# A hybrid decoder step on one core: where the SBUF arrays begin

## The reference

```python
h = rmsnorm(x, w_norm_mix)
proj = jnp.einsum('bld,de->ble', h, w_in)                  # 2048 -> 6160
o_r, s_ret = retention_chunkwise(q_r, k_r, v_r, s_ret0)
o_g, s_gla = gla_chunked(q_g, k_g, v_g, log_a, s_gla0)
x = x + jnp.einsum('ble,ed->bld', jnp.concatenate([o_r, o_g], -1), w_out)

q = jnp.einsum('td,de->te', rmsnorm(x, w_norm_ffn), w_pq)  # product-key queries
s1, s2 = q_first @ sub_keys1, q_second @ sub_keys2         # 128 + 128 keys, 8 heads
eidx, gate = top 16 of the 16 x 16 best sums, softmax
u = u_tab[eidx]
act = gelu(einsum('thkd,td->thk', u, xb))
out = einsum('thk,thkd->td', gate * act, v_tab[eidx])
y = rmsnorm(x + out, w_norm_final)
```

## Time and profile before

| | us |
|---|---|
| median of 3 runs | 3749.38 |
| lowest, highest | 3748.39, 3750.2 |
| the profiled execution | 3746.15 |
| its span, first to last instruction | 3744.4 |
| TensorE busy | 3542.5 (95%) |
| VectorE busy | 2554.4 (68%) |
| ScalarE busy | 1285.9 (34%) |
| mean granted TensorE clock | 0.964 |

### The profile page before, as it was taken

One profiled execution on the slowest core, in us unless ns is written; L12 is line 12 of the kernel. 1 busy time (PEld: TensorE's weight loads), 2 busy tenths in 40 slices (PEclk: granted clock), 3 DMA queues, 4 the chain that ended last, 5 costly groups with the idle time before them and its releaser, 6 DMA issues. The chain is left out here.

```text
span 3744.4 us, 50131 instructions
## 1 busy us (share of the span) xinstructions
PE 3542.5 (95%) x19479; PEld 3299.2 (88%) x19479; DVE 2554.4 (68%) x3619; ACT 1285.9 (34%) x1610; POOL 927.2 (25%) x609
## 2 busy tenths in 40 slices
PE   8999999676997998999999999999899999999996
PEld 6888888555786878999999999999899999999996
DVE  4112221786323216999999888887789899898997
ACT  5112221333322313323325777774222222222222
POOL 0000000000000000033333333432445445454452
PEclk9999999677998999999999999999999999999998
DMA  5222330543523405487888999999898998989986
GB/s 205 90 112 109 118 114 26 187 149 110 214 87 141 150 33 202 171 326 306 321 327 327 383 386 381 385 387 371 338 370 351 377 357 360 367 351 377 360 344 246
DMA packets 187000, 965.64 MB, mean 258 GB/s; under 512 B 18658, under 2 KB 61346, under 8 KB 86099
## 3 DMA queue, kind: packets, MB, share of 16 engines
q1 hardware_dynamic: 108082, 506.07, 35.7%
q0 software_dynamic: 61264, 426.27, 29.4%
q10 hardware_dynamic: 17488, 31.06, 2.3%
HBM read 865.77 MB, written 97.55 MB: 257 GB/s over the span
## 5 line engine op out<-in xcount | busy, mean ns | idle before, releaser
L1802 PE MATMUL hidden_hp<-dense_hi,units_whi 128*128 128x384 f32 x2048 | 696.6, 340 | 2.5 <-ACT units_whi L1565 2.5
L1803 PE MATMUL hidden_hp<-dense_lo,units_whi 128*128 128x384 f32 x2048 | 688.7, 336 | 0.0
L2284 PE MATMUL outputs_vp<-outputs_w_hi,units_whi 128*128 128x384 f32 x2032 | 679.0, 334 | 0.5 <-DVE units_wlo L1569 0.4
L2286 PE MATMUL outputs_vp<-outputs_w_hi,units_wlo 128*128 128x384 f32 x2032 | 678.7, 334 | 0.0
L2285 PE MATMUL outputs_vp<-outputs_w_lo,units_whi 128*128 128x384 f32 x2032 | 678.7, 334 | 0.0
L1565 ACT CAST units_whi<-units_raw 128x2048 fp32r<-128x2048 f32 x214 | 410.8, 1920 | 768.5 <-PE outputs_vp L2286 609.2
L1744 POOL DMA_INDIRECT hidden_row<-u_rows,expert_ids x192 | 367.4, 1914 | 999.5 <-DVE dots L2027 629.3
L1569 DVE TENSOR_TENSOR units_wlo<-units_raw,units_whi 128x2048 fp32r<-128x2048 f32 x214 | 489.9, 2290 | 102.1 <-ACT units_whi L1565 100.7
L2220 DVE SCALAR_TENSOR_TENSOR accg<-outputs_row,outputs_w_op,accg 128x2048 f32<-128x2048 f32 x192 | 450.9, 2349 | 51.1 <-DMA outputs_row<-v_rows,outputs_id 48.4
L2027 DVE CUSTOM_DVE_ANT_0 hidden_row<-hidden_row,hidden_h_row 128x2048 f32<-128x2048 f32 x192 | 436.7, 2290 | 70.9 <-DMA hidden_row<-u_rows,expert_ids 68.4
L2082 POOL DMA_INDIRECT outputs_row<-v_rows,outputs_id x192 | 319.6, 1664 | 525.3 <-DVE accg L2220 476.4
(11 more groups left out here) (366 smaller groups left out, 4821.2 us busy)
## 6 DMA issues: line engine op xcount, KB each, us to landing
units_raw<-v_units SPq DMA_DIRECT2D x128, 1024.0 KB
units_raw<-u_units SPq DMA_DIRECT2D x86, 1024.0 KB
in_proj_raw<-w_in SPq DMA_DIRECT2D x48, 1024.0 KB, 5.9
hidden_raw<-u_units SPq DMA_DIRECT2D x42, 1024.0 KB
hidden<-hidden_hid SPq DMA_DIRECT2D x128, 192.0 KB
gate_mat<-units_big SPq DMA_DIRECT2D x12, 2048.0 KB, 22.6
units_big<-hidden SPq DMA_DIRECT2D x16, 1536.0 KB
units_big<-gate_mat SPq DMA_DIRECT2D x16, 1536.0 KB
```

Of the source, the lines that this page charges most:

```text
L1802: mm(o, un.hi[s][:, x, :], h_hi[:, x, :], start=x == 0, stop=False)
L1803: mm(o, un.hi[s][:, x, :], h_lo[:, x, :], start=False, stop=False)
L2284: mm(o, un.hi[x][:, at, :], W_hi[s][:, e, :], start=e == 0, stop=False)
L2286: ins = mm(o, un.lo[x][:, at, :], W_hi[s][:, e, :], start=False, stop=e == CH - 1)
```

## The change

`squares` becomes a view of an array of 32 words, 128 bytes, so everything behind it begins 32 bytes later. On the right side an array `edge` of 32 bytes is made first, so the two `dense` arrays begin 32 bytes earlier. The instructions on each engine and their order are the same as before.

```diff
-        ident, squares = sb("ident", [P, P]), sb("squares", [P, D // NB, TILES])
+        ident = sb("ident", [P, P])
+        squares = sb("squares", [P, 32])[:, 0:D // NB * TILES].rearrange("p (b t) -> p b t", t=TILES)
...
         with ExitStack() as rows:
+            rows.enter_context(nc.sbuf_tensor("edge", [P, 8], F32, side="right"))
             dense = [rows.enter_context(nc.sbuf_tensor(f"dense_{p}", [P, KT, ND], F32R, side="right")) for p in ("hi", "lo")]
```

## The result

The changed kernel has a median of 3754.76 us against 3748.44 for the kernel before, measured beside it in 19 runs each; the ratio is 1.0019 with a 95% interval of 1.0012 to 1.0026. So the change costs about 7 us, 0.19%: inside the forecast's own range (3742 to 3756), but the forecast said that nothing would be measured, and the interval leaves out 1. The runs also lie further apart than before: 3751.19 to 3764.62 us against 3744.09 to 3751.87.

The account below looks back on a forecast made before the run. TensorE, busy for 3542.5 of 3744.4 us, was taken as the bound, with VectorE and DMA close behind. The four terms summed to 0, so 3749 us, unchanged; own range 3742 to 3756, range that should hold the time 3722 to 3760.

Parts of the forecast that it names:

- Term 1: Full-precision matrix multiplies on TensorE, some 2,800: placement costs 0; even 1 ns each would be 3 us.
- Term 2: Rounded 4-byte multiplies of projections, hidden and output stages, 16,700: gain bounded at 179 us, loss put at 0, taken as 0.
- Term 3: VectorE and ScalarE operations: placement costs 0 in both directions; 2 ns per ScalarE instruction would be 3 us.
- Term 4: DMA loads and stores: taken as 0, with at most 2.6 us of gain counted, in the query loads.
- A: Rival: the fixed part of the rounded multiplies, 10.7 ns each, is all placement; faster, 3610 us; chance 0.07.
- B: Rival: a ninth of the rounded multiplies' 10.7 ns goes, eight 64-byte pieces instead of nine; 20 us faster, 3729 us; chance 0.15.
- C: Rival: mixer slower, its sample-state buffers losing their multiple of 64, transfers a ninth longer; 11 us, 3760 us; chance 0.07.

Follow-up runs that it names:

- e6_gap128: Kernel before with the two dense arrays 128 bytes lower, so the distance to the units changes in the hidden stage; 3760.8 us, ratio 1.0030.
- e8_outputs_gap64: Kernel before with a spare array of 192 bytes, putting the output stage's moving operands 64 bytes below the place of their weights; 3756.17 us, ratio 1.0015.
- e3_both_zero: The change with 224 instead of 32 bytes at the right end, so units and dense both begin at 0 (mod 256); 3746.69 us, again 3745.84 us.
- e9_weights64: Kernel before with only the rounded and rest weights (units_whi, units_wlo) moved up by 64 bytes; 3773.30 us, ratio 1.0053.

## Why the prediction was wrong, by its steps

**Term 1** (full precision, 0) was right: the changed kernel has L1404 at 32 past a multiple of 64 and L1389 on one, and nothing moved. The earlier trace rows again (ns minimum/median/maximum):

```profile
L1404 PE MATMUL mixer_zo<-mixer_S,mixer_qm x128: 379/379/687, 693.6 to 885.9; 128*64 128x256 f32 x128
L1389 PE MATMUL mixer_st<-mixer_v_g,mixer_klr x32: 379/379/379, 742.5 to 917.5; 128*128 128x256 f32 x32
```

**Term 2** (rounded type, taken at 0 on both sides) is the step that failed. I bounded the gain with care and put the loss at 0 with the sentence that "what changes is only a start address and both placements cost the same in term 1". Two things are wrong in it. It looks at each operand by itself, although the address table beside the diff shows that the two operands of the hidden stage went opposite ways, from 224 and 224 to 192 and 0. And term 1 could not exclude a loss that the rounded type alone has. It does hold the distance: L1389's operands stood at 224 and at 32 (mod 256), L1404's both at 192, and both ran at 0.216 us, so full precision feels neither this distance nor the place. But of the rounded multiplies all 16,700 had a distance of 0 (mod 256) in the kernel before, so its trace had no case to bound the loss by, and where there is none, 0 is no bound. The term taken at 0 measures 2.16 ns on each of the hidden stage's 6144 multiplies and 1.6 on 576 of the queries', 14 us, of which 9 to 10 show. Of the working for the bound, the observation that rounded multiplies are more exposed than full-precision ones was sound; I used it for a gain only.

**Term 3** (VectorE, ScalarE, 0): right. L1569 is at 2289 ns after 2290, the ScalarE copy L1823 still takes 587. **Term 4** (DMA, 0 to 2.6 us), taken at 0: nothing speaks against it. The 1 MB loads of the input projection land after 5.5 instead of 5.9 us, and TensorE waits 20.6 instead of 23.4 us for the queries' rows, but kernels that leave all arrays at the left end where they were differ by as much (`e6_gap128` 5.3 and 19.7 us, `e8_outputs_gap64` 6.1 and 21.8), so the placement is not needed to explain it. The mask moved off its multiple of 256 lands after 4.7 us, before 4.6.

```profile
in_proj_raw<-w_in SPq DMA_DIRECT2D x48, 1024.0 KB, 5.5
...
mixer_S<-state_ret POOLq DMA_DIRECT2D x4, 1024.0 KB, 10.4
ret_s<-mixer_S POOLq DMA_DIRECT2D x4, 1024.0 KB, 5.4
...
mixer_keep<-const_keep SPq DMA_DIRECT2D x1, 256.0 KB, 4.7
```

**The rivals.** A and B (the 14 ns that every rounded multiply takes beyond its columns belong to the placement) fall: six distances, and a distance of 0 at two different places, gave the hidden stage no mean gap below 173.3 ns, and the outputs and the input projection, moved from 224 to 0, kept 173.3 and 226.9. B's picture of one piece of 64 bytes less per operand fell with `e3_both_zero`, where every operand has one less and the gap is unchanged. C (slower, in the mixer) had the right sign and the wrong place: the sample states load in 10.4 us after 10.8, and the mixer keeps its time (TensorE busy 76.41 of 100 us from 800 to 900, before 76.42). That the time fell inside the range was luck: the forecast's own 3742 to 3756 was its room for noise, the 3760 at the upper end stood there for C, with 0.07, and the loss that happened had no rival and no price.

The sentence on what would make the prediction wrong named the right sign, a start-to-start time of the rounded multiplies that moves by more than half a nanosecond, and that is where it was found. But the lines named for it, those of the output stage and the input projection, kept theirs; it was the hidden stage, which I had not named, that moved.

## What to carry to other kernels

When arrays are moved, compare the two operands of each heavy instruction with each other, not each with a rounder number; here keeping the distance (mod 256) was worth 7 us, and the multiple of 64 nothing that could be measured. Two allocators, or two ends of one, drift apart by a padding word in either. A pad at the left end moves its arrays up and one at the right end moves its arrays down, so equal pads do not cancel, they add: 32 and 32 bytes are the change, which lost, and 32 and 224, which make 256 together, are `e3_both_zero`, which did not. And judge a pipelined engine by its start-to-start time and its count in a fixed stretch: the mean busy time rose by 2 ns in kernels whose pace had not changed.

## What the runs showed of the hardware

- The rounded 4-byte multiplies of this kernel run at 173.3 ns for 384 columns when weights and moving operand begin at the same byte (mod 256), at 0 as at 224. With the moving operand 64 or 128 bytes below they lose up to 3.4 ns (2%); at 64 that was so with the weights at 0, at 32 and at 224. With it 32, 96 or 192 below they lose 0.2 ns at most. The full-precision ones kept 0.216 us from start to start (256 columns) at distances of 0 and 64. The queries' 512-column ones lose 1.6 ns at 64 bytes and 4.9 to 5.8 at 32, 96, 128 and 192.
- At 64 bytes the hidden stage has three paces, 173.3, 174.7 and 176.7 ns, each kept through one or many units of 48 multiplies; at 128 bytes two close ones, 176.0 in 115 of the 128 units and 175.5 in 11. In the output stage the same distance gave executions from 3747 to 3769 us of one program (`e8_outputs_gap64`), and with both stages from 3756 to 3779 (`e9_weights64`). A spread like that came with an address here.
- The Trainium skill ("TensorE: Matmul & The Clock Gate", section "Step-by-step: what each phase is for") says that TensorE reads weights and moving data through two independent ports, so that loading the next weights takes no read bandwidth from the running multiply. By that, where the weights lie should not matter to the multiply. The runs do not agree for this type: moving the weights alone by 64 bytes cost 25 us in the median (`e9_weights64`). That the two reads collide in SBUF, and settle in one of several rhythms, would fit the paces and the table; it is argued here and not shown, since no record shows a single read.
